# A mixture-of-experts tail in which the overflow block and the shared expert change places

## What is computed

```python
def swiglu(x, w1, w3, w2):
    return (jax.nn.silu(x @ w1) * (x @ w3)) @ w2

scores = sigmoid(xs @ router_w)          # 64 experts, 6 chosen per token
yg = lax.map(expert_block, (xg, blk_e))  # rows gathered by expert, blocks of 128
yg = yg.reshape(P, D) * slot_w[:, None]
routed = jax.ops.segment_sum(yg, slot_tok, num_segments=T + 1)[:T]
return routed + swiglu(xs, sh_w1, sh_w3, sh_w2)   # one shared expert
```

## Time and profile before

| | us |
|---|---|
| median of 3 runs | 2111.87 (2110.34 to 2111.94) |
| profiled execution, its own time | 2117.88 |
| span of the profiled execution | 2116.1 |
| TensorE busy | 1848.1 (87% of the span) |
| VectorE busy | 863.9 (41%) |
| GpSimd busy | 390.9 (18%) |
| 16 DMA engines, mean rate | 295 GB/s |

### The profile page before, as it was taken

The page is one execution under the profiler, slowest core; times in us unless marked ns, Lnnn a source line. Parts: engine busy times, 40 slices in busy tenths (PEclk is TensorE's granted clock), DMA queues, the critical chain, the costliest instruction groups (busy, mean ns, idle before and its releaser), DMA issues.

```text
span 2116.1 us, 30756 instructions
## 1 busy us (share of the span) xinstructions
PE 1848.1 (87%) x9520; PEld 983.5 (46%) x9521; DVE 863.9 (41%) x1525; ACT 458.6 (22%) x823; POOL 390.9 (18%) x577
## 2 busy tenths in 40 slices
PE   6999999886998789887988998877889799988996
PEld 3455555444544444444544443344445344444543
DVE  1556767567222222222116499575212222221226
ACT  4144444221111111111111554330111111110112
POOL 0010000011111111111105388012111111111113
PEclk9999999997999999999999999888999999999998
DMA  9488001474999999999988204355999999999955
GB/s 403 182 335 340 5 36 54 200 308 145 401 413 399 396 395 392 402 402 396 378 334 288 96 1 168 120 225 227 396 406 401 401 394 403 389 403 386 400 177 218
DMA packets 95681, 625.11 MB, mean 295 GB/s; under 512 B 16128, under 2 KB 16256, under 8 KB 57472
## 3 DMA queue, kind: packets, MB, share of 16 engines
q1 hardware_dynamic: 44640, 499.70, 58.7%
q0 software_dynamic: 26112, 79.72, 10.4%
q10 hardware_dynamic: 24864, 44.84, 5.8%
HBM read 563.38 MB, written 76.28 MB: 302 GB/s over the span
## 4 chain that ended last, share of the span: by engine, by line
PE 53%; DMA 28%; DVE 9%; POOL 5%; issue 3%; ACT 2%; SPq 0%; ACTq 0%; POOLq 0%; DVEq 0%
DMA ring<-in 26%; PE PS L1187 9%; PE PS L1181 8%; PE PS L1194 5%; PE PS L1208 3%; PE PS L1219 3%; POOL work L665 3%; PE PS L1408 3%; PE PS L1145 3%; PE PS L1098 3%; POOL work L633 3%; PE PS L1069 2%; PE PS L1136 2%; PE PS L1031 2%; PE PS L1108 2%
## 5 line engine op out<-in xcount | busy, mean ns | idle before, releaser
L1187 PE MATMUL PS<-ring,work 128*64 128x256 f32 x3360 | 418.8, 405 | 118.1 <-DMA ring<-in 101.1
L1187 PEld LDWEIGHTS PS<-ring,work 128*64 128x64 f32 x3360 | 259.6, 146 | 253.5 <-DMA ring<-in 105.2
L1597 DVE TENSOR_TENSOR work<-work,PS 64x256 f32<-64x256 f32 x105 | 44.4, 423 | 525.7 <-ACT work L732 525.7
L1181 PE MATMUL PS<-ring,work 128*128 128x512 f32 x400 | 182.6, 610 | 25.1 <-DMA ring<-in 19.0
L1194 PE MATMUL PS<-ring,work 128*64 128x512 f32 x840 | 203.3, 605 | 1.1 <-DVE work L1609 1.0
L585 POOL COPY col_i<-idx 128x1 int32 (+1 forms) x128 | 23.2, 181 | 794.8 <-PE PS L1219 787.4
L1603 DVE COPY work<-PS 128x1024 f32<-128x1024 f32 x128 | 156.7, 1224 | 11.8 <-PE PS L1219 8.0
L591 POOL DMA_INDIRECT work<-h_rows,col_i x128 | 125.3, 979 | 166.2 <-issue 166.2
L732 ACT ACTIVATE work<-PS 64x256 f32<-64x256 f32 x105 | 39.4, 376 | 511.2 <-PE PS L1187 511.2
L1219 PE MATMUL PS<-cst,work 128*128 128x128 f32 x1040 | 142.5, 281 | 6.8 <-DMA work<-h_rows,col_i 6.8
L1219 PEld LDWEIGHTS PS<-cst,work 128*128 128x128 f32 x1040 | 115.0, 142 | 59.9 <-issue 52.4
(11 more groups left out here) (264 smaller groups left out, 2243.4 us busy)
## 6 DMA issues: line engine op xcount, KB each, us to landing
ring<-in SPq DMA_DIRECT2D x147, 2048.0 KB, 18.2
ring<-in SPq DMA_DIRECT2D x132, 1024.0 KB, 18.6
y_rows<-sq POOLq DMA_DIRECT2D x2, 14336.0 KB, 61.0
y_rows<-work ACTq DMA_DIRECT2D x210, 128.0 KB
work<-in SPq DMA_DIRECT2D x11, 2048.0 KB, 9.0
ring<-in SPq DMA_DIRECT2D x3, 4096.0 KB, 16.3
y_rows<-work ACTq DMA_DIRECT2D x46, 256.0 KB
ring<-in SPq DMA_DIRECT2D x2, 3072.0 KB, 14.5
```

The source lines that it names most:

```text
L1181: last = mm(bank(6), lhs(c), w13(s)[:, :, c, :], start=(c == 0), stop=(c == DC - 1))
L1187: last = mm(bank(6)[64 * q:64 * q + 64, 0:F], lhs(c)[:, 0:64], w13(s)[:, q, c, :], start=(c == 0), stop=(c == DC - 1), tile_position=(0, 6 ...
```

## The change

The extra blocks run directly behind unit 63, ahead of all shared groups. For that the slots are swapped in part: the extra block's up weights go to the up part of slot 3 and its down weights stay in the down part of slot 2; the shared expert's up weights go to the up part of slot 2 and its down weights stay in slot 3. SyncE now issues unit 63's down weights, the extra block's up weights, its down weights, and last the shared expert's. The two shared products on VectorE move from ahead of turn 0 and turn 10 of the sums to ahead of turns 6 and 16.

```diff
--- before.py
+++ after.py
@@ -335,6 +335,7 @@
 
         SHARED, EXTRA = 3, 2
         CHUNK_BANK = (3, 0, 1, 2, 4, 5, 6, 7)
+        SHARED_TURN = (6, 16)
 
         def slot_of(u):
             return (3, 2, 0, 1)[u % RING]
@@ -447,10 +448,6 @@
                 def expert_down(e, s, done):
                     load_down(i, e, s, done)
 
-                def expert(e, s, done):
-                    expert_up(e, s, done)
-                    expert_down(e, s, done)
-
                 def refill_up(u, s):
                     sp.wait_ge(m["up_ps"], u - 3)
                     expert_up(ds(u, 1), s, w_in[s])
@@ -467,19 +464,21 @@
                 for u in range(E - 4, E - 1):
                     refill_up(u + 1, slot_of(u + 1))
                     refill_down(u, slot_of(u))
+                refill_down(E - 1, slot_of(E - 1))
+                sp.wait_ge(unit_rdy, i + 1)
                 sp.wait_ge(m["up_ps"], E - 3)
-                sp.dma_start(slot_ap(SHARED)[:, 0:UP], sh_w[i][:, 0:UP]).then_inc(sh_in, 16)
-                refill_down(E - 1, slot_of(E - 1))
-                sp.wait_ge(m["dn_ps"], E - 3)
-                sp.dma_start(slot_ap(SHARED)[:, UP:SLOT], sh_w[i][:, UP:SLOT]).then_inc(sh_in, 16)
-                sp.wait_ge(unit_rdy, i + 1)
-                sp.wait_ge(m["dn_ps"], E - 2)
                 many = nc.sync.value_load(unit_i[0:1, XMAX:XMAX + 1], min_val=0, max_val=XMAX)
                 with nc.sync.If(many > 0):
                     with nc.sync.Fori(0, many) as j:
                         sp.wait_ge(m["t_dn"], j + 1)
                         e = nc.sync.value_load(unit_i[0:1, ds(j, 1)], min_val=0, max_val=E - 1)
-                        expert(ds(e, 1), EXTRA, m["t_w"])
+                        expert_up(ds(e, 1), SHARED, m["t_w"])
+                        sp.wait_ge(m["dn_ps"], E - 2)
+                        expert_down(ds(e, 1), EXTRA, m["t_w"])
+                sp.wait_ge(m["up_ps"], E - 2)
+                sp.dma_start(slot_ap(EXTRA)[:, 0:UP], sh_w[i][:, 0:UP]).then_inc(sh_in, 16)
+                sp.wait_ge(m["dn_ps"], E - 3)
+                sp.dma_start(slot_ap(SHARED)[:, UP:SLOT], sh_w[i][:, UP:SLOT]).then_inc(sh_in, 16)
 
             for n in range(MODBUF):
                 load_mod(n)
@@ -783,7 +782,6 @@
                     a.wait_ge(sh_ps, 2 * blk + 1 + 5 * i)
                     A(shared[blk], bank(0), ACT.Silu).then_inc(sh_gate, 1)
 
-                shared_silu(0)
                 a.wait_ge(unit_rdy, i + 1)
                 many = nc.scalar.value_load(unit_i[0:1, XMAX:XMAX + 1], min_val=0, max_val=XMAX)
                 with nc.scalar.If(many > 0):
@@ -798,6 +796,7 @@
                                     .rearrange("p u d -> p (u d)"), yb[0]).then_inc(m["t_yout"], 16)
                         a.wait_ge(m["t_yout"], j * 16 + 16)
                         A(tick[0:1, i:i + 1], zero[0:1, 0:1], ACT.Copy)
+                shared_silu(0)
                 shared_silu(1)
 
             nc.scalar.preload_act_table(ACT.Sqrt)
@@ -1324,11 +1323,8 @@
 
                 def shared_up(blk, a):
                     for c in range(DC):
-                        last = mm(bank(3 * a), w13(SHARED)[:, a, c, blk * 128:blk * 128 + 128], hM[:, c, :], start=(c == 0), stop=(c == DC - 1))
+                        last = mm(bank(3 * a), w13(EXTRA)[:, a, c, blk * 128:blk * 128 + 128], hM[:, c, :], start=(c == 0), stop=(c == DC - 1))
                     last.then_inc(sh_ps, 1)
-
-                pe.wait_ge(sh_in, 32 * (i + 1))
-                shared_up(0, 0)
 
                 many = nc.tensor.value_load(unit_i[0:1, XMAX:XMAX + 1], min_val=0, max_val=XMAX)
                 with nc.tensor.If(many > 0):
@@ -1337,13 +1333,15 @@
                         rows_tr(0).then_inc(m["t_xgT_ps"], 1)
                         pe.wait_ge(m["t_xgT_ev"], j + 1)
                         pe.wait_ge(m["t_w"], j * 32 + 32)
-                        up_mm(lambda c: xgT[0][:, c, :], EXTRA).then_inc(m["t_up"], 1)
+                        up_mm(lambda c: xgT[0][:, c, :], SHARED).then_inc(m["t_up"], 1)
                         pe.wait_ge(m["t_act"], j + 1)
                         act_tr(0).then_inc(m["t_actT_ps"], 1)
                         pe.wait_ge(m["t_actT_ev"], j + 1)
                         pe.wait_ge(m["t_yev"], j + 1)
                         pe.wait_ge(m["y_ev"], E)
                         down_mm(0, EXTRA).then_inc(m["t_dn"], 1)
+                pe.wait_ge(sh_in, 32 * (i + 1))
+                shared_up(0, 0)
                 shared_up(0, 1)
                 pe.wait_ge(sh_gate, 1 + 2 * i)
                 shared_up(1, 0)
@@ -1768,11 +1766,10 @@
                     dve.wait_ge(sh_gate, blk + 1 + 2 * i)
                     V.tensor_tensor(shared[blk], shared[blk], bank(3), ALU.mult).then_inc(sh_act, 1)
 
-                shared_product(0)
                 for n in range(TT * K):
                     t, q = n // K, n % K
-                    if n == 10:
-                        shared_product(1)
+                    if n in SHARED_TURN:
+                        shared_product(SHARED_TURN.index(n))
                     dve.wait_ge(comb_in[n % 6], 16 * (n // 6 + 1 + i * TT * K // 6))
                     weight = wk[:, q * TT + t:q * TT + t + 1]
                     if q == 0:
```

## The result

The changed kernel takes 2119.16 us (median of 7 runs, 2117.16 to 2123.43), the one before 2111.94 (7 runs, 2108.98 to 2117.48): a ratio of 1.0033, 95% interval 1.0017 to 1.0049, which is +7 us (+3.6 to +10). Forecast were 2115.0, a range of 2108 to 2120, and "the same" as the likeliest. The time lies in the range, on its slow side; by the bound of 0.2% the change is slower, the case that had 0.32. (One execution of the kernel before, beside r9 and r10, took 7679.19 us and is left out of their ratios.)

The account below looks back on a forecast made before the run. The prediction took TensorE's products racing weight loads as the bound. Terms: 2.8 - 4.5 + 2.0 = +0.3 us in layer 0, 2.2 + 0.6 = +2.8 in layer 1, together +3.1, from 2111.87 to 2115.0 us; range 2108 to 2120.

Parts of the forecast that it names:

- the same: Verdict that the change is too small to see, within about 0.2% (2107.6 to 2116.1 us); chance 0.58.
- the case that had 0.32: Verdict that the changed kernel is measurably slower, beyond about 0.2%; chance 0.32.
- Product 1's turn, +2.8 and +2.2: Shared product 1 on VectorE starts later, so TensorE's last tile's transposes come +2.8 us in layer 0, +2.2 in layer 1.
- the step: Product 1 starts where turn 15 ends, 10.66 and 10.75 us later in the sums than at turn 10.
- the slack of 0.98 and 1.63 us: Time TensorE had to spare before the last tile's transposes, layers 0 and 1; deducted from product 1's delay.
- Strand A 6.9 us earlier: Extra block, store, 24 gathers and 24 sums start 6.9 us earlier in both layers, one shared group's time.
- the two strands: Behind unit 63: the rows' gathers and sums, and TensorE's shared groups, down products and transposes; they meet at the last tile's transposes.
- Unit 63's weights, -4.5 us: Unit 63's down weights issued ahead of 2 MB end TensorE's wait: -4.5 us in layer 0, nothing in layer 1.
- Rival 2: Slower: unit 63 gains nothing, held by its weights or the copy behind an unlanded store; sum +5.6 us, 2117.5; chance 0.14.
- nothing in layer 1: Issuing unit 63's down weights earlier gains nothing in layer 1, where nothing is waited for.
- The extra block's store, +2.0 us: In layer 0 the store is issued amid loads and lands later: +2.0 us, bounds 0 and +4.5.
- The clock, +0.6 us: Longer idle stretches lower TensorE's clock, slowing layer 1's shared down products as in layer 0: +0.6 us; 13.8 at full speed.

Follow-up runs that it names:

- r9: Changed kernel with product 1 ahead of turn 10 and ScalarE's wait for the even units' stores moved behind the extra block's silu: 2105.76 us, ratio 0.9956 to the kernel before.
- r10: Changed kernel with product 1 ahead of turn 10 instead of 16, run beside r9: 2107.78 us, ratio 0.9970 to the kernel before.
- r3: Kernel before with one line changed, product 1 ahead of turn 16 instead of 10: 2132.38 us, ratio 1.0089, +18.8 us.
- r8: Kernel before, unedited, run again for a second profiled execution: 2114.72 us in one execution.
- r1: Changed kernel, unedited, run again: 2118.58 us, ratio 1.0030 to the kernel before, +6.3 us.
- r4: Kernel before with only unit 63's down weights issued ahead of the shared expert's up weights on SyncE: 2113.44 us, ratio 1.0000.

## Why the prediction was right or wrong

**Product 1's turn, +2.8 and +2.2: the mechanism right, the size unproven to the microsecond.** TensorE became what ends both tails, and turns 12 to 16 move the time about as the step says. It priced r3 at 18.8 us, as measured, but that exactness is luck: the interval is 6 us wide, and both of its terms were read off one execution. By the step product 1 starts 19.76 + 10.66 = 30.4 and 19.88 + 10.75 = 30.6 us after the first gather; the four tails of the changed kernel have 28.1, 28.2, 28.9 and 31.7. And the slack of 0.98 and 1.63 us that it deducts wasn't there in r8.

**Strand A 6.9 us earlier: right**, and of use only to whoever doesn't wait. In layer 1 the first gather comes 21.38 us after the start of unit 63's down products in both profiles of the changed kernel, and 28.29 before; in layer 0 23.81 and 24.83, for the reasons below. The swap gives 12.5 us when both versions have turn 16, and about 7 when both have turn 10 (0.9962 and 0.9970), since the two strands then end together.

**Unit 63's weights, -4.5 us: mis-sized.** The term assumed that layer 0 would be as layer 1 with the weights there. Measured in the trace, 1075.62 to 1083.68 is 8.06 us (r1: 8.01), against 11.33, 10.74 and 9.64 in the old order: -1.6 to -3.3; in the medians of r4, 0 within 2. Rival 2's mechanism, the copy behind an unlanded store, did about half of its harm: ScalarE's wait came to light when the weights' wait went. The prediction's "nothing in layer 1" also rests on one execution: r8 has a wait of 1.50 us there.

**The extra block's store, +2.0 us: right in kind, too large.** It lands in 4.01 us in the first profile (r1: 2.90) against 2.65 before: +1.4 and +0.3. Chain in order of time, changed kernel:

```profile
1103.07 4.01 DMA y_rows<-work
```

**Left out: the extra block's silu.** The prediction looked at what the block's loads and gather need and not at ScalarE's wait ahead of its loop. Unit 63's down products to the block's took 14.44 us in layer 0 (r1: 14.88) and 13.38 in layer 1: +1.1 and +1.5, and in r1 the down products behind it took 5.40 us instead of 3.70: +1.7 more. The rule of the Trainium skill that the prediction weighed ("DMA: Bandwidth & Descriptors", Queues, rings and completion order: the semaphore comes after all earlier writes of that DMA engine) bears on this wait too, and these times agree with it: a store of unit 62 issued in the midst of loads landed after 12.94 us in r1's chain, while the lone store of the extra block in layer 1 took 2.65. No run isolates the rule.

**The clock, +0.6 us: not seen.** The down products to the transposes take 16.04 and 15.33 us (r1: 16.40 and 15.66), before 16.17 and 15.53. In the twelve profiles, idle stretches of 3.0 to 14.4 us ahead of the shared down products cost 1.5 to 3.0 us over the 13.8 at full speed, in no order of their length; those of 0.8 to 1.5 us there cost none.

Sum, with the forecast 5.0 for product 1 and what was measured for the rest: 5.0 - 2.5 (the middle of 1.6 and 3.3) + 0.9 + 1.3 + 0.9 (r1's slow down products in one of two) = +5.6 us, against +6.3 to +7.2 in the medians. That it comes so near is no proof of the 5.0. From the start of unit 63's down products to the residual's first instruction, the two tails together take 142.9 us in the mean of the three profiles of the old order with turn 10 (before, r8, r4) and 148.9 in the mean of the changed kernel's two: +6.0, where the terms behind unit 63 add up to 5.0 + 0.9 + 1.3 + 0.9 = +8.1. Less the 2.5 of unit 63 that leaves +3.5. Single tails of one kernel differ by up to 3.8 us, so the profiles can't settle the size; the medians can only say that it is a loss. The range held in part by luck: against the forecast of +3.1 this sum has +2.0 at unit 63 and +2.2 for the silu and the slow products behind it, which were left out, and -1.1 at the store and -0.6 at the clock, which offset some of that.

## What to carry to other kernels

When work is moved from one strand to behind another, look at the instruction on which the strands meet and at which engine carries it: a product of 0.68 us queued behind an unrelated, slow stream on an in-order engine cost more than all of the swap's gain. Place such a product at the first turn by which its input is ready; here two turns too early cost nothing that the medians show (10 against 12), six too late 19 us. And when a wait goes, ask what lay under it: here a wait for a store on ScalarE, twice.

Two profiled executions side by side are not a measurement: this pair had the wrong sign. Compare a stretch over several executions before giving a difference in it a cause.

## What the hardware showed that was not expected

The 24 gathers of 512 KB took 35.5 us between first and last issue in one execution of the kernel before and 32.7 in another (layer 0), in both with next to no other transfer under way (10.93 of the 10.95 MB moved in 1116 to 1152 of the first are the gathers'). TensorE's low clock sometimes comes only after work has resumed: in r9 unit 63's down products began at a granted clock of 1.00 and ran at 0.50 in 1086 to 1088, behind idle stretches of 1.06 and 0.68 us, while in the changed kernel's first profile the same products ran at full speed behind 0.88 and 0.83.
